# Gathering the second half of an expert pair's features behind the first weight unit instead of ahead of it

## The reference, cut to what matters

```
tokens = (xl * (1.0 + sc2) + sh2).reshape(B * S, D)
...
probs = softmax(logits).reshape(T, N_GROUPS, EXPERTS_PER_GROUP)   # 4 groups of 4
g = argmax(gscore); idx = top 2 within the group
...
expert: (silu(xb @ wg[e]) * (xb @ wu[e])) @ wd[e]                 # all 1024 x 1024, float32
out[token] += weight * expert(token)
xl = layer_norm(ALPHA * xl + (1 + g2) * out)
```

## Time and profile before

| | us |
|---|---|
| three runs | 1267.38, 1271.48, 1271.94 |
| median | 1271.48 |
| the profiled execution | 1269.37 |
| its span | 1267.6 |
| TensorE busy | 1140.6 (90% of the span) |
| VectorE busy | 358.9 (28%) |
| ScalarE busy | 165.1 (13%) |
| weights and other data moved | 479.40 MB, mean 378 GB/s |

### The profile page before, as it was taken

How to read it: one execution, slowest core, us unless ns; L and a number is a source line. 1 busy time by engine, 2 the same in 40 slices (tenths; PEclk the granted TensorE clock), 3 DMA queues, 4 the chain that set the end, 5 groups by cost and what they waited for, 6 DMA issues and landing times.

```text
span 1267.6 us, 12326 instructions
## 1 busy us (share of the span) xinstructions
PE 1140.6 (90%) x5284; PEld 507.5 (40%) x5284; DVE 358.9 (28%) x733; ACT 165.1 (13%) x398; POOL 15.9 (1%) x28
## 2 busy tenths in 40 slices
PE   4989699879899999999999998899999999999995
PEld 1544254444534433334333335633433333433331
DVE  1358889853211121111111113311111111111113
ACT  0110122342310000001000002400100000100000
POOL 0000000000000000000000001000000000000000
PEclk8989899789999999999999999999999999999999
DMA  9698787843799999999999999799999999999993
GB/s 376 248 331 292 307 314 282 336 162 141 325 430 426 429 428 427 428 428 428 426 429 427 428 425 422 311 429 427 428 429 427 427 427 428 428 427 429 427 427 165
DMA packets 37694, 479.40 MB, mean 378 GB/s; under 512 B 5723, under 2 KB 6875, under 8 KB 8581
## 3 DMA queue, kind: packets, MB, share of 16 engines
q1 hardware_dynamic: 31984, 433.64, 81.3%
q0 software_dynamic: 2880, 41.94, 8.9%
q10 hardware_dynamic: 2772, 2.99, 0.8%
HBM read 475.41 MB, written 1.05 MB: 376 GB/s over the span
## 4 chain that ended last, share of the span: by engine, by line
PE 71%; DVE 13%; DMA 10%; issue 2%; ACTq 2%; ACT 2%; DVEq 0%
PE ps L827 51%; PE ps L819 5%; PE ps L835 5%; DMA ring<-in_mod_w 4%; DMA ring<-in_moe_wu 3%; PE ps L687 2%; ACTq L999 2%; DVE ring L1258 2%; PE ps L590 2%; DVE work L1571 2%; DVE extra L1258 2%; DMA ring<-ring 2%; DVE work L1575 1%; DVE modp L1258 1%; PE ps L843 1%
## 5 line engine op out<-in xcount | busy, mean ns | idle before, releaser
L827 PE MATMUL ps<-ring,tra 128*64 128x512 f32 x2048 | 446.7, 594 | 2.1 <-ACT tra L1133 1.1
L827 PEld LDWEIGHTS ps<-ring,tra 128*64 128x64 f32 x2048 | 146.0, 137 | 298.5 <-issue 294.7
L827 PE MATMUL ps<-ring,work 128*64 128x512 f32 x1024 | 228.7, 598 | 29.2 <-DVE work L1571 29.2
L827 PEld LDWEIGHTS ps<-ring,work 128*64 128x64 f32 x1024 | 83.1, 137 | 154.1 <-issue 117.3
L1566 DVE TENSOR_TENSOR work<-ps,work 128x512 f32<-128x512 f32 x32 | 22.1, 691 | 279.4 <-ACT work L1140 279.4
L1140 ACT ACTIVATE work<-ps 128x512 f32<-128x512 f32 x32 | 19.1, 597 | 536.7 <-PE ps L827 536.7
L835 PE MATMUL ps<-work,extra 64*128 64x512 f32 x256 | 65.2, 629 | 21.0 <-DVE work L1575 21.0
L1133 ACT ACTIVATE tra<-ps,cols 128x128 f32<-128x128 f32 x128 | 48.1, 456 | 243.7 <-PE ps L819 243.7
L1569 DVE TENSOR_TENSOR work<-work,ps 128x512 f32<-128x512 f32 x32 | 22.0, 686 | 180.9 <-PE ps L827 180.9
L819 PEld LDWEIGHTS ps<-extra,xn 128*128 128x128 f32 x512 | 62.2, 199 | 25.6 <-issue 22.7
L590 PE MATMUL ps<-ring 128*128 128x512 f32 x128 | 59.8, 622 | 13.0 <-ACT ring L1029 13.0
(11 more groups left out here) (182 smaller groups left out, 711.4 us busy)
## 6 DMA issues: line engine op xcount, KB each, us to landing
ring<-in_moe_wg SPq DMA_DIRECT2D x64, 2048.0 KB, 23.2
ring<-in_moe_wu SPq DMA_DIRECT2D x64, 2048.0 KB, 22.6
ring<-in_moe_wd SPq DMA_DIRECT2D x64, 2048.0 KB, 22.2
ring<-in_mod_w POOLq DMA_DIRECT2D x20, 2048.0 KB, 8.7
ring<-in_attn_wqkv SPq DMA_DIRECT2D x5, 2048.0 KB, 12.8
ring<-in_mod_w SPq DMA_DIRECT2D x4, 2048.0 KB, 20.0
ring<-in_attn_wo SPq DMA_DIRECT2D x2, 2048.0 KB, 10.6
ring<-in_tokens SPq DMA_DIRECT2D x2, 1024.0 KB, 18.5
```

The costliest lines, as they stand in the source:

```text
L827: last = mm(ps[SLOTS * h:SLOTS * h + SLOTS, b, :], lhs(k0 + k), w[:, k, h * NB:(h + 1) * NB], start=(k0 + k == 0), stop=(k0 + k == KT - 1) ...
```

## The change

Half 1 of the first pair's features is no longer gathered in the loop ahead of the experts. The call moves into `expert`, behind the matmuls of unit 0 (gate 0) of the layer's first expert. Banks, semaphores and the waits that stand in the code stay as they are; what is queued on ScalarE, VectorE and SyncE doesn't change.

```
                         if e2 == 0 and (b, n) == (0, 1):
                             pe.wait_ge(sem("xg_copied"), 4 * (gq + 2 * pr_ + 2))
                         two_halves(4 + b, x_in, ring_unit(v + 2 * b + n), 4 * n).then_inc(sem("unit_used"), 1)
+                        if e == 0 and (b, n) == (0, 0):
+                            gather(7, 1).then_inc(sem("gather_done"), 1)
...
                 pe.wait_ge(sem("sgat_ready"), PAIRS * layer + 1)
-                for b in range(2):
-                    gather(6 + b, b).then_inc(sem("gather_done"), 1)
+                gather(6, 0).then_inc(sem("gather_done"), 1)
                 pe.wait_ge(sem("ssc_ready"), NE * layer + 1)
                 turn_weights().then_inc(sem("sw_turned"), 1)
```

## The result

| | median us | ratio to before, 95% interval |
|---|---|---|
| before, 17 executions | 1267.44 | |
| changed, 17 executions | 1274.56 | 1.0050 [1.0036, 1.0064] |

The ratio stands for 6.3 us (4.6 to 8.1); the forecast was 4.1. One execution of the changed kernel (1560.57 us) was disturbed and is left out of the ratio. The time lies in the stated range; the ratio lies on the bound of 0.5% itself, between "no change" (0.78) and "slower" (0.20). That 1274.56 is within 1.1 us of the forecast 1275.6 is luck: the forecast started from the median of three runs, 1271.48, which is 4.0 us above the median of 17, and its difference was too small by a third. The profiled execution took 1275.13 us with a span of 1273.3, 5.7 us over the span of before.

The account below looks back on a forecast made before the run. TensorE was taken to bound layer 0, and TensorE and the transfers to end layer 1 almost together. 2.6 us for layer 0 plus 1.5 for layer 1 on 1271.48 gave 1275.6 us, range 1272.0 to 1279.5.

Parts of the forecast that it names:

- no change: Whole kernel: a difference from before within about 0.5%, 6.4 us; chance 0.78.
- slower: Whole kernel: slower than before by more than about 0.5%, 6.4 us; chance 0.20.
- The pauses: TensorE, each layer's first expert: idle about 1.4 us ahead of unit 0, 1.60 ahead of unit 1, which starts 2.61 late.
- Layer 0, +2.6: End of layer 0: TensorE is 2.61 us late, the last landing still comes before it is needed, so +2.6 us.
- Layer 1, +1.5: End of layer 1: of TensorE's 2.61 us, slack of 1.0 to 1.26 is eaten, leaving 1.35 to 1.6.
- "+1.0" for load 11: Weight load waiting for unit 1, layer 1: lands 1.0 us later than before.
- upper bound of 1.2: Load 11, layer 1: running alone, it lands 7.9 us after its issue, 1.2 us later than before.
- the last landing moves by about +1.0: Transfers of a layer: the stream closes again behind load 11, so its last landing is only about 1.0 us later.
- Rival 3: Transfers: load 11 lands 3 us late instead of 1.0 and the last landing decides, 1277.1 us; chance 0.08.
- The clock, 0 in the sum: Whole kernel: the sum of 1275.6 us includes no time for a clock falling in the new pauses.
- rival 1: Pause ahead of unit 1, both layers: the clock falls, 1.7 us each, giving 1279.0 us; chance 0.15.
- rival 2: Layer 0's expert 15 and half 0's gather: half-speed stretches go, 1.7 us each, giving 1272.2 us; chance 0.10.

Follow-up runs that it names:

- e3: The change made in layer 1 only, both halves gathered ahead in layer 0, against the kernel before: 1.0018.
- e11: The changed kernel with one unused 128x512 matmul in each of two idle times ahead of the first gather, against the kernel before: 1.0009.
- e9: The kernel before with one unused 128x512 matmul in each of two idle times ahead of the first gather, against it without them: 0.9957.
- e6: The changed kernel with up 0 as the second unit of each layer's first expert, loads in that order, against the kernel before: 1.0030.
- e7: The kernel before with only the weights' turn moved between the two gathers, both ahead of unit 0, against it unmoved: 0.9988.
- e10: The changed kernel measured again, against the kernel before: 1.0046.
- e1: The changed kernel with half 1 gathered twice, ahead of the weights' turn (unused) and behind unit 0, against the kernel before: 1.0051.
- e2: The change made in layer 0 only, both halves gathered ahead in layer 1, against the kernel before: 1.0027.
- e8: The changed kernel with a wait for each copied block and up 0 as second unit in the first expert, against the kernel before: 1.0014.

## Why the prediction was right, and where it was thin

- **The pauses** were right in place, size and releaser. Forecast: second unit late by 2.61 us. Measured at full clock: 2.78 (e3) and 2.76 (e11 against e9). The pause ahead of unit 0 is 1.38 us there, as forecast (about 1.4), and the one ahead of unit 1 is 1.59 (1.60).
- **Layer 0, +2.6**: 2.9 between e9 and e11. Right, a little low as the pauses were.
- **Layer 1, +1.5**: 1.7 in e3, 2.0 in e11. TensorE's slack was there, but the landings took a part of it back. The term "+1.0" for load 11 was too small, and so was its upper bound of 1.2: the load ran alone. In e11 it was issued at 825.7 and landed 8.0 us later, 22.6 us behind the layer's gather, against 822.0 + 9.3, or 21.0, in e9: 1.6 later. Further on the landings are later still: the one that the last up unit waits for comes 2.0 us later behind the gather in e11 (1238.49 - 811.12 against 1235.62 - 810.28), and in the profiled execution of the changed kernel load 11 is late by 3.5 and the last landing by 4.2. The step "the last landing moves by about +1.0" missed that; why the delay grows behind load 11 is open. So in e11 TensorE still waits 0.18 us ahead of the last up unit (0.96 in e9), and 2.76 less 0.78 is the 2.0 that reaches the end. Rival 3 had the right mechanism and, for the pauses alone, too high a price.
- **The clock, 0 in the sum.** The prediction gave a fall in a new pause a chance of 0.15 and left it out of the sum. The time at 1.2 GHz is 6.0 us more with the change, which can be worth up to 3. What it cost in the end is not measured well. The 6.3 us of the ratio less the 4.9 of the profiles leaves 1.4; by the means the change costs 6.1 us (0.9) without the filler and 5.8 (0.8) with it, a difference that can't be told from zero. I had looked for the clock behind the pause ahead of unit 1 (rival 1). There it never was in the traces shown: the clock is 1.00 behind it in the changed kernel, and units 1 to 3 take 10.52 us in every profile that shows them whole. In the profiled execution it is at unit 0, as the tail of the slow stretch that the earlier trace rows shows over half 0's gather. I read that row and used it only for the gather's length. Of rival 2, the part on expert 15 happened in that execution (7.09 us instead of 8.78), and its first gather started 1.9 us earlier than that of before (325.40 against 327.32). Both are chance, and by them the profile's difference is 5.7 us and not over 9.
- **The rule on the clock** of the Trainium skill ("TensorE: Matmul & The Clock Gate", section "A second HAM failure mode: psum-queue depth-cycling"): short idle times that come often make the clock swing. For a pause between full-speed work the traces here don't agree (pauses of 1.4 and 1.6 us in e11, clock kept). For idle times around small instructions they lean its way: filling them took the time at 1.2 GHz from 74.1 to 64.8 us and 0.43% off the kernel, though layer 1 of e6, e7 and e10 kept the clock with the same idle times unfilled.
- **The chances.** 0.78 on no change and 0.20 on slower suited a result of 0.50% only just; by the 4.9 us of the profiles it would have been 0.39%. With an interval of 0.36 to 0.64%, which side of 0.5% it fell on is luck.

Open is why the stretch is longer on average with the change. The pause alone isn't it: e1 has none there and averages 80.3 us at 1.2 GHz (1.1), e7's profile has a stretch over both gathers of layer 0 (3.78 and 2.95 us) with no pause between them, e2, e3 and e10 have it and kept unit 0 fast in their profiles, and e8, with short pauses, averages 78.0 (1.7). Single executions vary too much to settle it with a profile each.

## What to carry to other kernels

A piece of work that is moved off the path takes the cover it gave with it: ask what the other engine did beside it (here 1.5 us of copies, twice) before counting its own time as saved. Where a wait stands for four pieces and the consumer needs them one after another, wait for each: that alone took back the cost as far as it can be measured (1.0000 [0.9987, 1.0013]). And look at the idle times ahead of a slow-clock stretch; filling them with unused matmuls was worth more here than any reordering. Before reading a difference from two profiles, check that their slow stretches lie in the same places.

## What the runs showed of the hardware

- Sixteen gathering instructions took 2.05 us at 2.4 GHz and 3.78 us at 1.2 GHz; a weight unit 3.49 to 3.65, and 5.67 us when most of it ran at 1.2 GHz.
- A load of 2 MB into idle queues lands 7.7 to 8.0 us after its issue, while in a full stream one lands every 4.93 us. Load 11 issued 7.2 us behind load 10 still paid that, though load 10, which landed at 832.5, had less than a microsecond to go:

```profile
L400 SPq DMA_DIRECT2D ring<-in_moe_wd x1: 327/327/327, 831.8 to 831.8; - x1
...
DMA to landing us min/median/max: 7.7/7.7/7.7
```

- A pause of 1.4 to 1.6 us between full-speed matmuls left the clock at 2.4 GHz in e11. Behind ten small rank instructions with idle times of 0.76 and 1.37 us around them, unfilled, the clock was at 1.2 GHz in both layers of the kernel before, and at 2.4 GHz in layer 1 of e6, e7 and e10.
